# Two transformer blocks on one core: the next stage's first weight group begun between the last groups of the stage before

## The reference

```python
# first block
h = rms_norm(x, ln1); proj = h @ w_in
y_a = gated_deltanet(...) @ w_branch_a
y_b = moba_attention(...) @ w_branch_b
x = x + (sigmoid(gate_a) * y_a + sigmoid(gate_b) * y_b) @ w_out
h = rms_norm(x, ln2)
u = causal_dwconv(h @ w_up, ffn_conv, ffn_conv_bias)
x = x + (silu(u_gate) * u_val) @ w_down
x = rms_norm(x, final_norm)
# second block
h = rms_norm(x, attn_norm); z = h @ w_in_2
x = x + concat(pool_out, rwkv_out) @ w_out_2
h2 = rms_norm(x, mlp_norm)
x = x + square(relu(h2 @ w_ffn_up)) @ w_ffn_down
gate = sigmoid(rms_norm(x, ple_norm) @ w_ple_gate)
x = x + gate * (p @ w_ple_proj)
out = rms_norm(x, final_norm_2)
```

## Time and profile before

| | |
|---|---|
| median of 3 runs | 3005.49 us (3004.7 to 3008.99) |
| the profiled execution, its own time | 3005.16 us |
| its span in the trace | 3003.4 us |
| mean granted TensorE clock | 0.983 |
| TensorE matmul busy | 2919.1 us (97%) |
| VectorE, ScalarE, GpSimd busy | 1891.2 (63%), 1464.5 (49%), 174.6 (6%) |
| memory traffic | 482.19 MB, mean 161 GB/s |

### The profile page before, as it was taken

How to read it: one execution, slowest core, us unless ns; L and a number is a source line. 1 busy time by engine, 2 the same in 40 slices (tenths; PEclk the granted TensorE clock), 3 DMA queues, 4 the chain that set the end, 5 groups by cost and what they waited for, 6 DMA issues and landing times.

```text
span 3003.4 us, 54743 instructions
## 1 busy us (share of the span) xinstructions
PE 2919.1 (97%) x23504; PEld 2852.2 (95%) x23504; DVE 1891.2 (63%) x2130; ACT 1464.5 (49%) x1891; POOL 174.6 (6%) x143
## 2 busy tenths in 40 slices
PE   8999999999999999999999999999899999999998
PEld 7988889999999999999998998898899999999997
DVE  6467765455666666666666677557655555655565
ACT  5356555444454444444446456554544444444464
POOL 0010110000000000000001012021000000000000
PEclk9999999999999999999999999989999999999999
DMA  6645533665556656665665532313466666656554
GB/s 213 185 119 155 155 91 100 183 183 175 188 178 189 184 177 187 185 182 176 183 187 160 165 92 85 113 50 94 135 183 183 183 183 183 183 181 186 184 170 134
DMA packets 252100, 482.19 MB, mean 161 GB/s; under 512 B 16945, under 2 KB 22321, under 8 KB 251729
## 3 DMA queue, kind: packets, MB, share of 16 engines
q1 hardware_dynamic: 251856, 478.68, 52.9%
HBM read 476.53 MB, written 2.10 MB: 159 GB/s over the span
## 4 chain that ended last, share of the span: by engine, by line
PE 83%; DVE 8%; ACT 4%; issue 3%; DMA 2%; POOL 0%; DVEq 0%; SPq 0%; ACTq 0%; POOLq 0%
PE psm L186 75%; PE psb L186 7%; DVE ar L224 2%; ACT ar L202 2%; DVE ar L214 1%; DVE slo L214 1%; DMA raw<-in_w_in 1%; PE psb L189 1%; ACT shi L202 1%; DVE x L214 1%; DVE gl L224 1%; ACT gh L202 0%; DVE ar L228 0%; ACT L202 0%; ACT hh L202 0%
## 5 line engine op out<-in xcount | busy, mean ns | idle before, releaser
L214 DVE TENSOR_TENSOR slo<-raw,shi 128x1024 fp32r<-128x1024 f32 (+1 forms) x901 | 1128.8, 1258 | 714.5 <-ACT shi L202 712.6
L202 ACT ACTIVATE shi<-raw 128x1024 fp32r<-128x1024 f32 (+1 forms) x901 | 947.6, 1054 | 1163.9 <-PE psm L186 947.5
L186 PE MATMUL psm<-gh,shi 128*128 128x256 f32 x3664 | 1052.1, 287 | 20.4 <-DVE slo L214 16.9
L186 PE MATMUL psm<-gl,shi 128*128 128x256 f32 x3664 | 1041.0, 284 | 0.0
L186 PE MATMUL psm<-gh,slo 128*128 128x256 f32 x3664 | 1040.8, 284 | 0.0
L186 PE MATMUL psm<-hh,shi 128*128 128x256 f32 x3408 | 977.3, 287 | 18.4 <-DVE slo L214 9.8
L186 PE MATMUL psm<-hl,shi 128*128 128x256 f32 x3408 | 967.7, 284 | 0.0
L186 PE MATMUL psm<-hh,slo 128*128 128x256 f32 x3408 | 967.4, 284 | 0.0
L186 PEld LDWEIGHTS psm<-gh,shi 128*128 128x128 f32 x3664 | 706.5, 193 | 28.5 <-DVE slo L214 18.3
L186 PEld LDWEIGHTS psm<-gl,shi 128*128 128x128 f32 x3664 | 706.5, 193 | 1.0 <-issue 0.3
L186 PEld LDWEIGHTS psm<-gh,slo 128*128 128x128 f32 x3664 | 706.0, 193 | 0.3
(11 more groups left out here) (199 smaller groups left out, 1326.9 us busy)
## 6 DMA issues: line engine op xcount, KB each, us to landing
raw<-in_w_in SPq DMA_DIRECT2D x240, 512.0 KB, 3.7
raw<-in_w_up SPq DMA_DIRECT2D x176, 512.0 KB, 4.0
raw<-in_w_ffn_up SPq DMA_DIRECT2D x128, 512.0 KB, 3.8
raw<-in_w_ffn_down SPq DMA_DIRECT2D x128, 512.0 KB, 3.9
raw<-in_w_down SPq DMA_DIRECT2D x88, 512.0 KB, 4.6
raw<-in_w_out SPq DMA_DIRECT2D x64, 512.0 KB, 4.2
raw<-in_w_ple_gate SPq DMA_DIRECT2D x32, 512.0 KB, 4.3
raw<-in_w_branch_b SPq DMA_DIRECT2D x16, 512.0 KB, 3.9
```

The lines of the kernel that those rows point to most:

```text
L186: return self.issued(self.eng and self.eng.matmul(out, lhs, rhs, start=start, stop=stop, skip_group_check=True), cost)
L202: return self.issued(self.eng and self.eng.activation(out, in_, fn, scale=scale, **kw), cost)
L214: return self.issued(self.eng and self.eng.tensor_tensor(out, a, b, op), self.cost(out))
```

## The change

The plan now holds parts of groups: `group` takes `part`, the range of chunks. `lora`'s chunks 0 to 3 (2 tiles) come after `down` (10, 1), chunks 4 to 7 after `down` (10, 2), the other 4 tiles after `down` (10, 3). In the same way `fup` 0 comes in parts of 2, 2 and 4 tiles after `out2b` (3, 1), (3, 2) and (3, 3). A group that is open keeps its place in `psm`; the places are given out as they come free, so that the last two groups of the old stage take the other place, one after the other, and each waits for the eviction of the one directly before it.

```diff
+    def group(name, w, row, col, ncols, nk, kc=2, part=None):
+
+        first, last = part or (0, nk)
+        plan.append((name, [(w, row + 128 * k, kc, col, ncols) for k in range(first, last, kc)], first, last == nk))
...
                 group(("down", g - 1, f), io["w_down"][0], 512 * (g - 1), 512 * f, 512, 4)
-    group(("lora", 0), w_in2, 0, 4096, 288, 16)
+                if g == 11 and f in (1, 2):
+                    lora(4 * f - 4, 4 * f)
+    lora(8, 16)
...
-            group(("out2b", h, f), w_out2, 1024 + 256 * h, 512 * f, 512, 2)
+            out2b(h, f)
+            if h == 3 and f in (1, 2):
+                fup(0, (4 * f - 4, 4 * f))
...
-            group(("fup", g), io["w_ffn_up_2"][0], 0, 512 * g, 512, 16)
+            fup(g, None if g else (8, 16))
...
+        tiles, end, slot, before, owner, free = [], {}, {}, {}, [None, None], [0, 1]
+        for name, ts_, _, ends in plan:
             tiles += ts_
+            if name not in slot:
+                i = slot[name] = free.pop(0)
+                before[name], owner[i] = owner[i], name
+            if ends:
+                end[name] = len(tiles) - 1
+                free.append(slot[name])
...
-                            if i >= 2:
-                                pe.wait_ge(*evicted(plan[i - 2][0]))
+                            if before[name]:
+                                pe.wait_ge(*evicted(before[name]))
...
+                    while part and not known((dve_step, part(k - 1))):
+                        first_step()
...
                         group(("down", g - 1, f))
+                        if g == 11 and f in (1, 2):
+                            group(("lora", 0))
...
                     group(("out2b", h, f))
+                    if h == 3 and f in (1, 2):
+                        group(("fup", 0))
```

More of the change, by code:

```diff
@@ L378, in weight_plan, with lora, fup, out2b @@
     plan = []
-    def group(name, w, row, col, ncols, nk, kc=2):
-        plan.append((name, [(w, row + 128 * k, kc, col, ncols) for k in range(0, nk, kc)]))
+    def group(name, w, row, col, ncols, nk, kc=2, part=None):
+        first, last = part or (0, nk)
+        plan.append((name, [(w, row + 128 * k, kc, col, ncols) for k in range(first, last, kc)], first, last == nk))
+    def lora(first, last):
+        group(("lora", 0), w_in2, 0, 4096, 288, 16, part=(first, last))
+    def fup(g, part=None):
+        group(("fup", g), io["w_ffn_up_2"][0], 0, 512 * g, 512, 16, part=part)
+    def out2b(h, f):
+        group(("out2b", h, f), w_out2, 1024 + 256 * h, 512 * f, 512, 2)
     for g in range(6):
@@ L485, in build @@
         plan = weight_plan(io)
-        tiles, end, place = [], {}, {}
-        for i, (name, ts_) in enumerate(plan):
+        tiles, end, slot, before, owner, free = [], {}, {}, {}, [None, None], [0, 1]
+        for name, ts_, _, ends in plan:
             tiles += ts_
-            end[name], place[name] = len(tiles) - 1, i
+            if name not in slot:
[4 more added lines that the diff above has]
+                free.append(slot[name])
         NT = len(tiles)
         def psum(name):
-            return psm[:, place[name] % 2, :]
+            return psm[:, slot[name], :]
         def evicted(name):
@@ L665, in weights @@
                                 pe.wait_ge(dve_step, part(k))
-                            ah, al, first, last = h[:, o + k, :], l[:, o + k, :], k == 0, k == nk - 1
+                            ah, al, first, last = h[:, o + k, :], l[:, o + k, :], k == 0, ends and k == nk - 1
                             if name in (("moba", 4), ("moba", 5)):
@@ L2127, in vector_program @@
             progs |= {("epi", ("branch_a", g)): merge_a(g) for g in range(4)}
-            progs |= {("epi", n): add_x(n) for n in place if n[0] in ("out", "down", "out2a", "out2b", "fdn")}
+            progs |= {("epi", n): add_x(n) for n in end if n[0] in ("out", "down", "out2a", "out2b", "fdn")}
             progs |= {("epi", (n, g)): conv_up((n, g)) for n in ("up", "uv") for g in range(11)}
@@ L2372, in plan_order @@
             programs = (tensor_program(pe), scalar_program(act), vector_program(dve), gpsimd_program(gpsimd), sync_program(sync))
-            order, lanes, want, first = [], [[], [], [], []], [[], [], [], []], []
-            low, building, pairs, whole = [], [0], [], []
+            order, lanes, want, first, parts = [], [[], [], [], []], [[], [], [], []], [], list(plan)
+            low, building, pairs, whole, placed = [], [0], [], [], [0]
             def advance(name):
@@ L2473, in group @@
             def group(name):
-                i, j = place[name], end[name] - len(plan[place[name]][1])
-                for ti, (_, _, kc, _, n) in enumerate(plan[i][1]):
-                    j += 1
+                got, ts, k, ends = parts.pop(0)
+                assert got == name, (got, name)
+                part = operand(name)[3]
+                for ti, (_, _, kc, _, n) in enumerate(ts):
+                    j = placed[0]
+                    placed[0] += 1
                     at = lo_done.time(j)
-                    if ti == 0 and i >= 2:
-                        freed = evicted(plan[i - 2][0])
+                    if k == 0 and before[name]:
+                        freed = evicted(before[name])
                         until(freed)
                         at = max(at, freed[0].time(freed[1]))
+                    k += kc
+                    while part and not known((dve_step, part(k - 1))):
+                        first_step()
                     ready(at)
@@ L2494, in group @@
                         advance("hi")
-                    if ti == len(plan[i][1]) - 1:
+                    if ends and ti == len(ts) - 1:
                         epilogue(name)
```

6 lines of the change are left out of this document (3 added, 3 removed).

## The result

The changed kernel takes 3002.57 us (median of 20 runs, 2997.05 to 3006.20), the kernel before, run beside it, 3006.72 us (median of 20, 2997.76 to 3009.56): 4.2 us less, a ratio of 0.9986 with a 95% interval from 0.998 to 0.9992. It lies within the 0.2% that the prediction called "no change", on the fast side. 3000.0 us was forecast, with 5.5 us less; the measured time lies outside the 2998 to 3001.5 us given to the forecast itself and inside the whole range of 2995.4 to 3003.8.

The account below looks back on a forecast made before the run. TensorE, busy 97% of the span, bounds the kernel; only its waits at the two places can go. Gains of 1.5 + 4.0 = 5.5 us from 3005.16 give 2999.7, 3000.0 with 0.33 to the median; range 2998 to 3001.5, whole range 2995.4 to 3003.8.

Parts of the forecast that it names:

- The ledger of the first place: `down` 10 to the norm, step by step: the listed waits, about 7.3 us together, with the norm's matmuls starting at 1623.5.
- Rival 1: First place: VectorE gets ahead of GpSimd's second addition and the clock holds; 8.8 us gained, 2996.7 us; chance 0.2.
- rival 4: First place: the clock falls in the short waits from 1601.6 on and stays low; slower, 3010 us; chance 0.05.
- The clock's part: First place, norm: 0.9 us off the gain, for a fall costing 1.2 to 1.4 us about two times in three.
- Gain 2.4 us: First place, before the clock deduction: `rkv` starts at 1627.0 instead of 1629.4; only what is late at the end counts.
- TensorE waits again in `rkv`: A sign, behind the first place, that the prediction is wrong; no size given.
- Second place: `out2b` 3 and `fup` 0: waits of 1.5 and 2.4 us go, at most 0.5 to 1.4 us before tile 8.
- Rival 2: First place: the norm starts after 1625.9, so no gain is left; second place gives 3 us; 3002.5 us; chance 0.2.
- Rival 3: Second place: `pt` and quarter 3 come late and the norm waits too; 1 us gained in all, 3004.5; chance 0.08.
- the first term: First place, up to `rkv`'s start: 1.5 us gained, which is 2.4 us less 0.9 us for the clock.
- the second term: Second place, up to the end of `fup` 0: 4.0 us gained, from 3.8 to 4.6 us.

Follow-up runs that it names:

- e3: The change with VectorE's sixteen scalings of `x` dealt out, two behind each `rkv` tile, instead of one piece; 2994.28 us against 3005.42 for the kernel before (0.9966).
- e1: The change at the first place alone, `fup` 0 left whole; 3007.37 us against 3005.42 for the kernel before (1.0003).
- e4: The change with `pt` loaded 29 us earlier, without waiting for `out2b` (3, 3); 3005.5 us, 1.0002 of the kernel before.
- e11: The change with the end of `rkv`'s norm forced forward on VectorE, scalings still in one piece; 2999.87 us against 3007.02 for the kernel before (0.9982).
- e2: The change at the second place alone, `lora` left whole; 3002.67 us, 0.9988 of the kernel before.
- e9: e3 with the additions of squares for `rkv`'s norm moved from GpSimd to VectorE; 2994.14 us against 3005.49 for the kernel before (0.9953).
- e10: e3 with the last eviction of each old group put ahead of one low half on VectorE; 2995.35 us, 0.9967 of the kernel before.
- e12: e9 with the additions of squares for `fup`'s norm also moved to VectorE; 2989.59 us against 3007.02 for the kernel before (0.9941).
- e8: The change at the second place alone, with VectorE's scalings of `x` spread over `rkv`'s tiles; 2996.68 us against 3005.49 for the kernel before (0.9967).
- e13: e9 with the end of `rkv`'s norm set early, as in e11; 2995.65 us against 3007.02 for the kernel before (0.9967).
- e14: e12 without the first place of the change, `lora` whole behind `down`; 2997.0 us against 3004.74 for the kernel before (0.9974).
- e7: The kernel before with only VectorE's scalings of `x` spread over `rkv`'s tiles; 2998.93 us against 3005.49 for the kernel before (0.9978).

## Why the prediction was right in the whole and wrong in its parts

**The ledger of the first place held.** Forecast were waits of 1.6 us ahead of `down` (10, 3), 1.4, 0.8 and 0.9 ahead of `lora`'s tiles 6 to 8, and 2.6 ahead of the norm, whose matmuls were to start at 1623.5. Measured: 1.38, 1.22, 0.56, 0.82, 2.53 and 1623.59. Rival 1 needed the chain quicker and rival 4 the clock low for long; neither was so.

**The clock's part was too small.** I took off 0.9 us, as two falls in three. The norm's sixteen matmuls took 5.38 us, against 3.45 in the chain of before and 3.69 in e3: 1.7 to 1.9 us. Behind a wait of 2.5 us the norm was slow in the change, e1, e4 and e11 (5.38, 5.28, 5.10, 5.17) and not in e3 (3.69). The clock fell in four executions of five, so the two times in three were not far off; the price was. The 1.4 and 1.2 us of a fall were read from stretches that begin or end inside the low part. The four stretches of 4 us from 1604 to 1620 of the kernel before, with granted clocks of 0.68, 0.89, 0.96 and 0.61, give 1.7 us for each fall.

**The step that failed is the one that carried "Gain 2.4 us" on to the end**: that only what is late at `rkv`'s start counts, and that behind it VectorE's work costs nothing. TensorE ran out of work at 1660.63 (1667.27 - 6.64), before at 1661.11 (1664.36 - 3.25): of the 1.5 us only 0.5 reached this point (2.4 less the clock's 1.9). Then the low half that it needed came 2.91 us later than before, and everything behind it with it. 0.7 us of this came back, since the clock was low there before as well and more of the low part now passed in the wait: from the end of the wait to the third group's eviction it was 40.33 us before and 39.62 after. That makes the 2.3 us. I had costed the loads and the waits up to the norm, and left out that the norm's end and `lora`'s epilogue are steps of VectorE too, whose places in its queue are given relative to tiles. The prediction named "TensorE waits again in `rkv`" among the signs of an error, but no rival had it with a price. Its price can be read from the trace of before: VectorE there was 3.25 us too late at this tile with a piece of 8.3 us ahead of it, so TensorE has to meet each microsecond by which the piece moves. e11, which moves it back, and e3, which takes it apart, show this; 1.5 us forecast became 2.3 us of loss in the trace, and nothing (+0.03%, from -0.1% to +0.15%) in e1's runs.

**Second place: right mechanism, too large a term.** The 1.48 and 2.40 us went and the wait was ahead of tile 8, as forecast; it was 1.85 us, not 0.5 to 1.4. ScalarE got `pt` at 2154.10, which is 2152.1 on before's clock (this execution is 2.0 us later at `out2b` (3, 0)), where I had the load land at about 2151. The gain was 2.9 us instead of 4.0 (3.1 from the other starting point); e2's runs give 0.12% of 3005 us, 3.6.

**The rivals.** Rival 2's total of 3002.5 us is nearly what was measured, but its mechanism isn't: the norm started on time. Rival 3 had `pt` and the norm late together; the change has one of them, and e4 shows that the other waits right behind. That the total came out near, 4.2 us for 5.5, is in part luck: the first term had the wrong sign. Its error of 3.8 us by the distances and that of the second term, 1.1 us, would have left 0.6 us of gain; the runs show 3.6 us more than that, and most of the 3.6 stays unexplained.

## What to carry to other kernels

When a group is moved ahead in the order, list every step of the slower engines that is tied to it, not only up to the point where the group ends: an epilogue or a norm's end that slides by three tiles, as here, can hit a long piece of work behind it. After any edit, compare the whole order: e4, e9, e10 and e12 also moved the norm among TensorE's tiles, which the edit did not name. A piece of vector work several microseconds long ahead of a matmul operand is a loss to look for before any reordering: spreading it gave 6.6 us here by one line, more than the whole change. And one late input that is mended can show the next in line; look at who would be waited for 1 us later before mending it.

## What I had not expected of the hardware

One stretch behind both places decides most of the spread of the runs. Between the evictions `x<-x,psm` that begin at 1962.95 and 2040.92 in the kernel before, TensorE's clock is at its lower level for 20 to 27 us in some executions and for 3 to 7 in others, with the same instructions. The stretch 1976:1984 of the change, then of e2:

```profile
1976.00:1984.00 8.00, 8.00 (x38) 7.16 (x38) 1.70 (x4) 2.31 (x7) 4.26 (x6) 0.50 0.09 35
```

```profile
1976.00:1984.00 8.00, 8.00 (x55) 6.80 (x55) 2.77 (x7) 3.46 (x10) 5.52 (x8) 0.84 0.00 0
```

The way from the one eviction to the other took 76.8 to 79.1 us in nine of the fourteen profiled executions (before, the change, e1, e4, e8, e9, e12, e13 and e14) and 70.3 to 72.0 in five (e2, e3, e7, e10, e11). That is 7 us, more than the change is worth, and what decides it is open. Spans of single executions, e2's 2992.1 against 3001.0 say, therefore tell nothing about an edit here until this stretch is taken out of them.

GpSimd's additions are the other surprise in size: taking two of 2.4 us off an engine that is busy 6% of the time, and giving them to one that is busy 63%, was worth 1.7 to 2.2 us at the second place by the distances. The fastest kernel of the study, e12, has both with the scalings spread: 0.9941 of the kernel before.
